# Spacing the last group's routing pieces and the final norm's steps between expert pairs

## The chip, the cores and the metric

The kernel runs on one core of one Trainium2 chip. Its time is the device time of one launch in microseconds (us), taken as the median of several runs. Engine names in the rows: PE is TensorE, DVE is VectorE, ACT is ScalarE, POOL is GpSimd, SP is SyncE; a small q behind a name is that engine's queue of DMA issues.

## The reference

One layer of a decoder trunk, in float32, for 1024 prompt tokens and 8 sample tokens of width 1024. The two groups share all weights.

```
n  = rmsnorm(x, g_mix) * (1 + sc1) + sh1            # adaLN
z  = n @ w_in                                        # conv branch, gMLP branch, two gates
x  = x + gt1 * ((sigmoid(g_a) * a + sigmoid(g_b) * b_br) @ w_out)
n2 = rmsnorm(x, g_ffn) * (1 + sc2) + sh2
q  = n2 @ w_q                                        # 8 heads, two half keys
s1, s2 -> top 16 of 128 each -> 256 sums -> top 16   # 128 experts per token
act = gelu(sum_d u_tab[eid] * n2)
x  = x + gt2 * sum_n (softmax gate * act)_n * v_tab[eid]_n
y  = rmsnorm(x, g_final)
```

The expensive part is the expert part. Every token reads 128 rows of `u_tab` and of `v_tab`, which lie side by side in memory as one row of 8 KB.

## The kernel before, in words

The tokens are cut into eight blocks of 128 (blocks 0 to 7) and one sample block of 8 (block 8). Three groups of blocks go through the dense front (norms, projections, convolution, gates, query, top 16): G1 is block 0, G2 is blocks 1 to 3, G3 (the last group) is blocks 4 to 8.

**Pairs.** The expert part is cut into pairs, counted by `at`. A pair is two gathers of 128 rows of 8 KB, 2 MB together. A block has 64 pairs (`PAIRS`), 32 for each half; the sample block has 4, ahead of block 7. That is 516 pairs: block 4 is pairs 256 to 319, block 5 is 320 to 383, block 6 is 384 to 447, the sample is 448 to 451, and block 7 is 452 to 515. For each pair:

- POOL issues two gathers into a slot (L1045, `fetch`). It first waits until PE has used the rows of the pair that had the slot before. Up to pair 255 there are three slots, from pair 256 (`WIDE_AT`) there are five.
- DVE multiplies each 128x1024 half by the token's vector and sums it (L1507, `dots`); ACT takes the gelu (L987); DVE makes the weights (L1524, `weigh`); PE multiplies the other half of the rows by them (L765, `value`), and so releases the slot.

**What stands between pairs.** Every engine's program is a fixed list in the order in which it is written. `beside_peer` (L370) writes it: `dots(at)`, `weigh(at)`, some steps of the fronts of G2 and G3 (over by pair 247), and then `extra(at)`. On DVE `extra` (L1608) issues three sorts of work:

- Routing pieces. `route` (L1432) turns the top-16 tables of one block into expert numbers and gates. It is a generator with ten pieces: piece 0 to piece 3 find the top 16 of 50 candidates for 8 heads; pieces 4 to 7 (the heavy ones) each have three instructions over 128x1600 elements (L1464, L1467, L1469), and piece 7 adds 16 small copies of `eid` (`to_quads`, L1429); piece 8 sums the softmax; piece 9 scales and makes 16 small copies of `gate`. Block 4 is routed in the front of G3. `routing_3` routes block 5, block 6, the sample (plus one piece, `to_slots`) and block 7, 41 pieces. They stand behind 10 consecutive pairs from pair 256, 10 from pair 320, and 21 from pair 384.
- `take_acc` takes the sum of a half out of PE's accumulator, two pairs behind its end.
- `early_norm` does the final norm of the blocks that are done: eight `x2` steps (L1552, the residual sum), mean squares, root, eight `y` steps (L1563). One step stands behind each pair from pair 452.

ACT does the exponential of each routing at pairs that the table `exps` names, and `square` and `root` of the norm at pairs counted from `last_block`. SP waits for the last routing (L476), then reads the eight 512 KB blocks of `x1_rows` and the sample's rows back, as `early_norm` needs them, and writes each `y` out once it is ready (L484).

Of the kernel before, what the change touches and what calls it, by code (L numbers as in the profile page):

```python
# [29 lines left out]
NB = NP // P  # L30
# [18 lines left out]
PAIRS = NSLOT * P // (2 * P)  # L49
# [2 lines left out]
NPAIRS = NB * PAIRS + SPAIRS  # L52
SAMPLE_AT = (NB - 1) * PAIRS
ROUTE_PIECES = 10
HEAVY = 3
END_B = 60
END_C = 4 * PAIRS - 8
# [38 lines left out]
def half_start(h):  # L96

    return HALF * h + (SPAIRS if h >= 2 * (NB - 1) else 0)
# [18 lines left out]
def build(nc, t):  # L117
# [3 lines left out]
    with ctx:  # L121
# [3 lines left out]
        def part(area, at, *shape):  # L125
            names = "abc"[:len(shape)]
            spec = "p (%s) -> p %s" % (" ".join(names), " ".join(names))
            return area[:, at:at + int(np.prod(shape))].rearrange(spec, **dict(zip(names, shape)))
# [112 lines left out]
        def width(b):  # L241
            return P if b < NB else NS


        def group(n, blocks, tg, xn, tables):
            g = Group()
            g.n, g.blocks, g.nb, g.tg, g.xn = n, blocks, len(blocks), tg, xn
            g.nt = sum(width(b) for b in blocks)
            g.ng = g.nt // tg
            g.nf = sum(b < NB for b in blocks)  # L250
            g.np = g.nf * P
            g.S = {k: S[f"{k}{1 if n < 3 else 2}"] for k in group_names}
            g.S |= {k: S[f"{k}{n}"] for k in ("x_in", "out_x1")}
            g.base = totals(G1) if n == 2 else {}

            g.order = list(range(g.nb)) if n < 3 else [0, 1, 2, 4, 3]
            g.cand = part(tables, 0, g.nb * H, NC)
            g.cid = part(tables, g.nb * H * NC, g.nb * H, NC)
            g.posf = part(mbuf, 3200, g.nb * H, TOP) if n < 3 else part(mbuf, 0, g.nb * H, TOP)
            g.crep = part(mbuf, 3200 + 512, H, NC) if n < 3 else part(mbuf, 1024, H, NC)  # L260
            g.eq = eq if n < 3 else part(mbuf, 2048, 2, TOP, NC)
            g.gt1 = (gt1_a, gt1_b, gt1_c)[n - 1]
            return g
# [3 lines left out]
        G3 = group(3, list(range(NB1, NBT)), 260, xn2, wring)  # L267
# [68 lines left out]
        def front_weights(g):  # L336

            for work, idle in ((4 * CC * g.ng, 5), (2 * CC * g.ng, 5), (4 * g.nb, 12), (2 * g.nb, 5),
                               (3 * KC * g.ng, 5), (2 * g.ng, 17), (3 * KC * g.ng, 7), (8 * g.nb, 3)):
                if work == 4 * CC * g.ng:  # L340
                    yield from norm_steps(g)
                    yield from [1] * 5
                yield from [HEAVY] * work
                yield from [1] * idle
            yield from norm_steps(g)
            yield from [1] * 5
            yield from [HEAVY] * (2 * g.nb)
            yield from [1] * 3
            yield from [HEAVY] * (NCH * (2 * g.ng + 1))
            yield from [1] * (2 * g.ng + 1) * 3  # L350
# [38 lines left out]
        def x1_again(b):  # L389
            return mbuf[:, b * D:(b + 1) * D] if b < NB1 else wring[:, (b - NB1) * D:(b - NB1 + 1) * D]  # L390
# [8 lines left out]
        def _(sp):  # L399
# [4 lines left out]
            def load(n):  # L404
                kind, src, col, _, _ = pieces[n]
                if user_ahead[n] is not None:
                    done, count = pieces[user_ahead[n]][3:]
                    sp.wait_ge(done, count)
                sp.dma_start(home(n), src[col]).then_inc(s_piece[slot_of[n]], 16)
# [78 lines left out]
        def _(pe):  # L488
# [292 lines left out]
            def begin(at):  # L781
                b, _, m = place(at)
                if b is None:
                    while made[0] < min(NS, max(3, 2 * m + 2)):
                        sample_x(made[0])
                        made[0] += 1
# [4 lines left out]
        def _(act_):  # L791
# [12 lines left out]
            def replicate(h, c):  # L804

                b, half = h // 2, h % 2
                j, q = 2 * half + c // NQ, c % NQ
                if c == 0:
                    g = G1 if b == 0 else G2 if b < NB1 else G3
                    act_.wait_ge(*g.to("n2_done", b - g.blocks[0] + 1))  # L810
                    if h >= 2:
                        act_.wait_ge(S["dots"], half_start(h - 2) + HALF)
                xn = xn1[:, b, :] if b < NB1 else xn2[:, b - NB1, :]
                made = ac(xr[QUAD * q:QUAD * (q + 1), j, :], xn[QUAD * j:QUAD * (j + 1), :], ACT.Copy)  # L814
                if c == 7:
                    made.then_inc(S["xr_ready"], 1)
# [172 lines left out]
            def square(n):  # L989

                b = finals[n]
                w = width(b)
                act_.wait_ge(S["x2_done"], n + 1)
                if n >= 2:
                    act_.wait_ge(S["fin_sq"], n - 1)
                ac(part(w2, 0, 2, D)[0:w, n % 2, :], x1_again(b)[0:w, :], ACT.Square, accum_out=stat[0:w, 0, n:n + 1]
                   ).then_inc(S["fin_sq"], 1)

            def root(turn, lo, hi):
                act_.wait_ge(S["fin_ms"], turn)  # L1000
                ac(stat[:, 1, lo:hi], stat[:, 0, lo:hi], ACT.Sqrt).then_inc(S["fin_root"], 1)

            exps = {PAIRS + ROUTE_PIECES * i + 6: G2 for i in range(2)}
            exps |= {at + 6: G3 for at in (4 * PAIRS, 5 * PAIRS, 6 * PAIRS, 6 * PAIRS + ROUTE_PIECES + 1)}
            copies = {half_start(h - 1) + 20 + c: (h, c) for h in range(2, 2 * NB) for c in range(8)}
            last_block = half_start(2 * (NB - 1))

            def extra(at):
                if at in exps:
                    next(exps[at].numerators)  # L1010
                if at in copies:
                    replicate(*copies[at])
                n = at - last_block - 4
                if 0 <= n < NB:
                    square(n)
                if n == NB + 1:
                    root(1, 0, NB)

            beside_peer(gelu, lambda at: None, {2: front(G2), 3: front(G3)}, extra)
            square(NB)  # L1020
            root(2, NB, NBT)
# [51 lines left out]
        def _(dve):  # L1073
# [457 lines left out]
            def take_acc(n):  # L1531

                dve.wait_ge(S["rows_used"], ends[n] + 1)
                for h in range(2):
                    part_ = slice(512 * h, 512 * (h + 1))
                    if n == 2 * (NB - 1):
                        out, acc, by = xn2[0:NS, 4, part_], ps[QUAD * h:QUAD * h + NS, 0, :], gts[:, part_]
                    else:
                        b, half = (n - (n > 2 * (NB - 1))) // 2, (n - (n > 2 * (NB - 1))) % 2
                        at = slice(2 * QUAD * half, 2 * QUAD * (half + 1))  # L1540
                        by_half = slice(2 * QUAD * h, 2 * QUAD * (h + 1))
                        out = (xn1[at, b, part_] if b < NB1 else xn2[at, b - NB1, part_])
                        acc, by = ps[by_half, half, :], gt2[by_half, part_]
                    last = v.tensor_tensor(out, acc, by, ALU.mult)
                last.then_inc(S["acc_read"], 1)
# [20 lines left out]
            def early_norm():  # L1566

                dve.wait_ge(S["x1_back"], 16 * NBT)
                dve.wait_ge(S["gfin_in"], 16)
                yield from gap(3)  # L1570
                dve.wait_ge(S["acc_read"], 2 * NB - 1)
                for n in range(NB):
                    x2(n)
                    yield
                yield
                mean_squares(1, 0, NB)
                yield from gap(2)
                dve.wait_ge(S["fin_root"], 1)
                rsqrt(0, NB)
                yield  # L1580
                for n in range(NB):
                    y(n)
                    yield
# [13 lines left out]
            def routing_2():  # L1597
                for i in (1, 2):
                    yield from route(G2, i)

            def routing_3():
                for i in range(1, 4):
                    yield from route(G3, i)
                yield from to_slots()
                yield from route(G3, 4)

            second, third, norms = routing_2(), routing_3(), early_norm()
            def extra(at):  # L1608
                if PAIRS <= at < PAIRS + 2 * ROUTE_PIECES:
                    next(second, None)  # L1610
                for b, count in ((4, ROUTE_PIECES), (5, ROUTE_PIECES), (6, 2 * ROUTE_PIECES + 1)):
                    if b * PAIRS <= at < b * PAIRS + count:
                        next(third, None)
                if at - 2 in ends:
                    take_acc(ends.index(at - 2))
                if at >= half_start(2 * (NB - 1)):
                    next(norms, None)

            dve.wait_ge(S["mask_made"], 1)
# [72 lines left out]
```

## Time and profile before

| | |
|---|---|
| median of 3 runs | 3551.34 us (3548.37 to 3553.54) |
| the profiled execution, its own time | 3556.78 us |
| its span | 3555.2 us |
| PE, DVE, ACT, POOL busy | 2051.7, 2448.6, 441.8, 1249.4 us |
| gathers (software queue) | 1082.20 MB of 1232.08 MB |
| share of the chain that ended last on DMA | 23% |

The execution has two regimes. Until about 2100 us the fronts of G2 and G3 run between the pairs, and no engine is full throughout. From there, in the last 17 of the 40 slices, only pairs, routing pieces and norm steps are left; DMA is full in most slices and below that in a few. A share over the whole span says little about the second regime, so it is read by stretches.

### The profile page before, as it was taken

How to read it: one execution, taken by the hardware profiler on the slowest of the kernel's cores; microseconds unless marked ns; L12 is line 12 of the kernel's file. 1: busy time of each engine (PE TensorE's matmuls, PEld its weight loads, DVE VectorE, ACT ScalarE, POOL GpSimd, SP SyncE). 2: the span in 40 equal slices, each digit the busy share in tenths (PEclk: the TensorE clock that was granted, in tenths of full speed). 3: DMA queues.
4: the chain of work that ended last, by engine and by line, in shares of the span. 5: the costliest groups of instructions: out<-in, count | busy, mean ns of one | idle time of the engine just before them, and what ended most of it. 6: DMA issues, size and time to landing. Idle time of an engine off the chain costs nothing. (4 is left out here: it accounts for less than half of the span.)

```text
span 3555.2 us, 28830 instructions
## 1 busy us (share of the span) xinstructions
PE 2051.7 (58%) x9548; PEld 995.9 (28%) x9548; DVE 2448.6 (69%) x6290; ACT 441.8 (12%) x1031; POOL 1249.4 (35%) x1046
## 2 busy tenths in 40 slices
PE   6873878986277777778688623333343333355333
PEld 4762444643144344455345300000000000000000
DVE  1447574479898796655768997766866697656665
ACT  1121101011111110110211011101010101011100
POOL 0001221222233433333434334544454444445343
PEclk9886988998588888899799855555555555555555
DMA  7734756798579999899999869999999998998998
GB/s 297 311 144 166 301 207 260 272 358 318 220 283 360 363 334 371 329 383 419 395 410 406 345 251 401 375 422 422 368 417 421 422 386 354 421 421 341 423 421 343
DMA packets 183925, 1232.08 MB, mean 347 GB/s; under 512 B 30512, under 2 KB 31152, under 8 KB 36320
## 3 DMA queue, kind: packets, MB, share of 16 engines
q0 software_dynamic: 148608, 1082.20, 75.9%
q1 hardware_dynamic: 35168, 148.05, 10.6%
q8 instruction: 75, 1.23, 0.1%
q14 instruction: 74, 0.61, 0.0%
HBM read 1221.14 MB, written 9.02 MB: 346 GB/s over the span
## 5 line engine op out<-in xcount | busy, mean ns | idle before, releaser
L1045 POOL DMA_INDIRECT big<-in_experts,eid x920 | 1112.0, 1209 | 2081.9 <-PE ps L765 1620.4
L1507 DVE SCALAR_TENSOR_TENSOR big<-big,xr 128x1024 f32<-128x1024 f32 x920 | 1113.6, 1225 | 525.3 <-DMA big<-in_experts,eid 520.2
L765 PE MATMUL ps<-big,wd 128*32 128x512 f32 x3680 | 726.2, 873 | 1089.8 <-DVE wd L1524 1085.2
L530 PE MATMUL ps<-big,wring 128*128 128x260 f32 (+2 forms) x2400 | 644.9, 423 | 81.5 <-issue 56.3
L530 PEld LDWEIGHTS ps<-big,wring 128*128 128x128 f32 x2400 | 447.6, 201 | 318.7 <-issue 166.1
L765 PEld LDWEIGHTS ps<-big,wd 128*32 128x32 f32 x3680 | 85.0, 127 | 1591.0 <-DVE wd L1524 1535.7
L987 ACT ACTIVATE gel<-act 128x2 f32<-128x2 f32 x516 | 105.7, 205 | 2569.9 <-DVE big L1507 2322.8
L1524 DVE TENSOR_SCALAR wd<-mask,gel,gate 128x32 f32<-128x32 f32 x1024 | 275.1, 363 | 152.3 <-ACT gel L987 141.5
L765 PE MATMUL ps<-w,wd 128*32 128x512 f32 x208 | 100.3, 1061 | 174.7 <-DVE wd L1524 170.8
L1205 DVE SCALAR_TENSOR_TENSOR arena<-arena,wdw 128x128 f32<-128x128 f32 (+2 forms) x360 | 182.9, 572 | 0.0
L682 PE MATMUL ps<-wring,mbuf 128*128 128x256 f32 (+1 forms) x528 | 128.6, 400 | 11.6 <-DMA wring<-in_w_out 6.3
L682 PEld LDWEIGHTS ps<-wring,mbuf 128*128 128x128 f32 (+1 forms) x528 | 96.0, 186 | 54.7 <-issue 28.8
L530 PE MATMUL ps<-arena,wring 128*128 128x260 f32 (+1 forms) x384 | 107.1, 422 | 0.0
L1045 POOL DMA_INDIRECT w<-in_experts,eid x52 | 57.2, 1100 | 130.3 <-PE ps L765 126.3
L765 PE MATMUL ps<-arena,wd 128*32 128x512 f32 x208 | 100.3, 1061 | 0.0
L1507 DVE SCALAR_TENSOR_TENSOR arena<-arena,xr 128x1024 f32<-128x1024 f32 x52 | 63.7, 1226 | 50.6 <-DMA arena<-in_experts,eid 50.6
L765 PEld LDWEIGHTS ps<-w,wd 128*32 128x32 f32 x208 | 10.2, 140 | 264.8 <-DVE wd L1524 259.2
L530 PEld LDWEIGHTS ps<-arena,wring 128*128 128x128 f32 x384 | 71.5, 190 | 37.9 <-issue 15.1
L1507 DVE SCALAR_TENSOR_TENSOR w<-w,xr 128x1024 f32<-128x1024 f32 x52 | 63.7, 1225 | 19.8 <-DMA w<-in_experts,eid 19.5
L1507 DVE DVE_READ_ACCUMULATOR big<-big,xr 128x1 f32 x920 | 76.8, 84 | 0.0
L1045 POOL DMA_INDIRECT arena<-in_experts,eid x52 | 68.6, 1319 | 15.9 <-issue 15.9
L814 ACT ACTIVATE xr<-arena 32x1024 f32<-32x1024 f32 x64 | 67.5, 1055 | 1.5
(219 smaller groups left out, 1881.0 us busy)
## 6 DMA issues: line engine op xcount, KB each, us to landing
wring<-in_w_in SPq DMA_DIRECT2D x40, 1024.0 KB
wring<-in_w_q SPq DMA_DIRECT2D x19, 1024.0 KB
big<-in_experts,eid POOLq DMA_INDIRECT x920
wring<-in_w_ada SPq DMA_DIRECT2D x12, 1024.0 KB
wring<-in_w_out SPq DMA_DIRECT2D x9, 1024.0 KB
big<-in_w_ada SPq DMA_DIRECT2D x6, 1024.0 KB, 6.9
xr<-in_w_ada SPq DMA_DIRECT2D x6, 1024.0 KB, 8.8
big<-in_w_in SPq DMA_DIRECT2D x4, 1024.0 KB, 14.7
```

Source lines behind the costliest of these rows:

```text
L530: mm = mmul(out, piece(n)[:, c, col:col + P], src[:, c, gi * tg:(gi + 1) * tg], start=(c == 0), stop=(c == k - 1))
L682: mm = mmul(ps[0:w, 2 + i % 6, 0:256], mT[:, c, cols(b)], piece(n + col)[:, c, :], start=(c == 0), stop=(c == KC - 1))
L765: mm = mmul(ps[QUAD * j:QUAD * (j + 1), half, :], wd[:, 2 * (at % 4) + jj, :], row(2 * slot + jj)[:, D + 512 * h:D + 512 * (h + 1)], start ...
L814: made = ac(xr[QUAD * q:QUAD * (q + 1), j, :], xn[QUAD * j:QUAD * (j + 1), :], ACT.Copy)
L987: ac(gel[:, c:c + 2], act[:, c:c + 2], ACT.Gelu).then_inc(S["gelu"], 1)
L1045: gp.indirect_dma_start(row(r), None, t["experts"], bass.IndirectOffsetOnAxis(ap=index, axis=0)).then_inc(s_row[r], 16)
L1205: ins = v.scalar_tensor_tensor(out=y, in0=aT[:, c, kk:kk + g.np], scalar=wdw[:, c, kk:kk + 1], in1=y, op0=ALU.mult, op1=ALU.add)
L1507: last = v.scalar_tensor_tensor(out=row(r)[:, 0:D], in0=row(r)[:, 0:D], scalar=1.0, in1=x, op0=ALU.mult, op1=ALU.mult, accum_out=act[:, c: ...
L1524: last = v.tensor_scalar(wd[:, c, :], mask[:], gel[:, c:c + 1], gate[:, b % 4, 2 * half + jj, m:m + 1], ALU.mult, ALU.mult)
```

## The change

The last group's 41 routing pieces no longer stand behind consecutive pairs in three bunches. One stands behind every fourth pair from pair 256 on (`ROUTE_STEP` = 4): block 5 at pairs 256 to 292, block 6 at 296 to 332, the sample at 336 to 372, `to_slots` at 376, block 7 at 380 to 416. The steps of the final norm stand behind every second pair from pair 452 (`NORM_STEP` = 2) instead of behind every pair, so the first `x2` is behind pair 458 instead of 455 and the last `y` behind 496 instead of 474. ACT's exponentials, squares and root move with them. No instruction is added or removed. From line 55 on, line numbers are two higher.

```diff
+ROUTE_STEP = 4
+NORM_STEP = 2
...
-            exps |= {at + 6: G3 for at in (4 * PAIRS, 5 * PAIRS, 6 * PAIRS, 6 * PAIRS + ROUTE_PIECES + 1)}
+            exps |= {4 * PAIRS + ROUTE_STEP * (at + 6): G3 for at in (0, 10, 20, 31)}
...
-                n = at - last_block - 4
-                if 0 <= n < NB:
-                    square(n)
-                if n == NB + 1:
+                n, rest = divmod(at - last_block - 1, NORM_STEP)
+                if rest == 0 and 3 <= n < NB + 3:
+                    square(n - 3)
+                if rest == 0 and n == NB + 4:
                     root(1, 0, NB)
...
-                for b, count in ((4, ROUTE_PIECES), (5, ROUTE_PIECES), (6, 2 * ROUTE_PIECES + 1)):
-                    if b * PAIRS <= at < b * PAIRS + count:
-                        next(third, None)
+                if at >= 4 * PAIRS and at % ROUTE_STEP == 0:
+                    next(third, None)
                 if at - 2 in ends:
                     take_acc(ends.index(at - 2))
-                if at >= half_start(2 * (NB - 1)):
+                if at >= half_start(2 * (NB - 1)) and (at - half_start(2 * (NB - 1))) % NORM_STEP == 0:
                     next(norms, None)
```

VectorE's list at two heavy routing pieces of block 5 before the change (`L1507 ... x2` and `L1524` are one pair; `mbuf`, `wring` and `eid_s` belong to the routing piece):

```order
L1464 TENSOR_TENSOR mbuf<-mbuf,iota 128x1600
L1467 TENSOR_TENSOR mbuf<-mbuf,wring 128x1600
L1469 TENSOR_REDUCE eid_s<-mbuf 128x32
L1507 SCALAR_TENSOR_TENSOR big,act<-big,xr 128x1024 x2
L1524 TENSOR_SCALAR wd<-mask,gel,gate 128x32 x2
L1464 TENSOR_TENSOR mbuf<-mbuf,iota 128x1600
```

The same two pieces on VectorE in the changed kernel:

```order
L1466 TENSOR_TENSOR mbuf<-mbuf,iota 128x1600
L1469 TENSOR_TENSOR mbuf<-mbuf,wring 128x1600
L1471 TENSOR_REDUCE eid_s<-mbuf 128x32
L1509 SCALAR_TENSOR_TENSOR big,act<-big,xr 128x1024 x2
L1526 TENSOR_SCALAR wd<-mask,gel,gate 128x32 x2
L1509 SCALAR_TENSOR_TENSOR big,act<-big,xr 128x1024 x2
L1526 TENSOR_SCALAR wd<-mask,gel,gate 128x32 x2
L1509 SCALAR_TENSOR_TENSOR big,act<-big,xr 128x1024 x2
L1526 TENSOR_SCALAR wd<-mask,gel,gate 128x32 x2
L1509 SCALAR_TENSOR_TENSOR big,act<-big,xr 128x1024 x2
L1526 TENSOR_SCALAR wd<-mask,gel,gate 128x32 x2
L1466 TENSOR_TENSOR mbuf<-mbuf,iota 128x1600
```

Between the two heavy pieces there was one pair and there are four now.

VectorE's list at the first steps of the final norm before the change, in block 7 (`L1552` is an `x2` step):

```order
L1552 TENSOR_TENSOR mbuf<-mbuf,xn 128x1024
L1507 SCALAR_TENSOR_TENSOR big,act<-big,xr 128x1024 x2
L1524 TENSOR_SCALAR wd<-mask,gel,gate 128x32 x2
L1552 TENSOR_TENSOR mbuf<-mbuf,xn 128x1024
L1507 SCALAR_TENSOR_TENSOR w,act<-w,xr 128x1024
```

The same steps on VectorE in the changed kernel:

```order
L1554 TENSOR_TENSOR mbuf<-mbuf,xn 128x1024
L1509 SCALAR_TENSOR_TENSOR big,act<-big,xr 128x1024 x2
L1526 TENSOR_SCALAR wd<-mask,gel,gate 128x32 x2
L1509 SCALAR_TENSOR_TENSOR big,act<-big,xr 128x1024 x2
L1526 TENSOR_SCALAR wd<-mask,gel,gate 128x32 x2
L1554 TENSOR_TENSOR mbuf<-mbuf,xn 128x1024
```

Two pairs stand between two steps instead of one, and the first step comes three pairs later.

## Rows read from the trace of the kernel before

**Rows 1.** The page: the span in 40 slices.

```profile
DMA  7734756798579999899999869999999998998998
GB/s 297 311 144 166 301 207 260 272 358 318 220 283 360 363 334 371 329 383 419 395 410 406 345 251 401 375 422 422 368 417 421 422 386 354 421 421 341 423 421 343
```

**Rows 2.** Stretches: length, PE, PEld, DVE, ACT, POOL busy, PEclk, DMA share, GB/s.

```profile
2285.00:2489.00 204.00, 79.31 (x328) 8.26 (x328) 124.70 (x248) 24.14 (x56) 96.61 (x82) 0.50 1.01 421
2164.70:2275.00 110.30, 38.32 (x160) 3.82 (x152) 92.77 (x233) 6.78 (x22) 49.59 (x39) 0.50 0.93 379
2496.90:2605.00 108.10, 38.36 (x160) 3.83 (x152) 92.16 (x232) 6.78 (x22) 48.81 (x39) 0.50 0.92 374
2827.20:2980.00 152.80, 50.17 (x212) 5.23 (x208) 141.36 (x365) 17.21 (x38) 67.21 (x51) 0.50 0.90 363
2980.00:3020.00 40.00, 12.83 (x56) 1.21 (x48) 18.93 (x37) 3.55 (x9) 15.68 (x14) 0.50 1.02 417
```

**Rows 3.** Stretches of block 5, L1507 alone, four records a pair: DVE busy, GB/s.

```profile
2496.90:2827.20 330.30, 156.69 (x256) 0.50 0.98 406
2497.00:2568.00 71.00, 24.01 (x40) 0.50 0.89 360
```

**Rows 4.** Timeline of one undisturbed pair: start, length, engine, instruction, [idle before, releaser].

```profile
3507.04 0.56 DVE L1524 TENSOR_SCALAR wd<-mask,gel,gate 128x32 f32<-128x32 f32 x2 [0.27 <-ACT gel L987]
3507.65 1.94 PE L765 MATMUL ps<-big,wd 128*32 128x512 f32 x8 [3.03 <-DVE wd L1524]
3508.01 1.23 DVE L1507 SCALAR_TENSOR_TENSOR big<-big,xr 128x1024 f32<-128x1024 f32 x1 [0.41 <-DMA big<-in_experts,eid]
...
3509.89 0.94 POOL L1045 DMA_INDIRECT big<-in_experts,eid  x1 [2.32 <-PE ps L765]
3510.50 1.23 DVE L1507 SCALAR_TENSOR_TENSOR big<-big,xr 128x1024 f32<-128x1024 f32 x1 [1.26 <-DMA big<-in_experts,eid]
...
3512.01 0.56 DVE L1524 TENSOR_SCALAR wd<-mask,gel,gate 128x32 f32<-128x32 f32 x2 [0.27 <-ACT gel L987]
```

**Rows 5.** Timeline of block 6's routing: a `take_acc`, heavy piece 5, the copies of piece 7.

```profile
2507.86 1.39 DVE L1544 TENSOR_TENSOR arena<-ps,gt 64x512 f32<-64x512 f32 x2
...
2531.87 1.82 DVE L1464 TENSOR_TENSOR mbuf<-mbuf,iota 128x1600 f32<-128x1600 f32 x1
...
2533.73 1.82 DVE L1467 TENSOR_TENSOR mbuf<-mbuf,wring 128x1600 f32<-128x1600 f32 x1
2534.26 2.11 POOL L1045 DMA_INDIRECT big<-in_experts,eid  x1 [5.28 <-PE ps L765]
2535.59 1.82 DVE L1469 TENSOR_REDUCE eid_s<-mbuf 128x32 f32<-128x1600 f32 x1
...
2554.71 3.05 DVE L1429 CAST eid<-eid_s 32x32 uint32<-32x32 f32 x16
```

**Rows 6.** Stretches of one pair each, L1507 alone: length, DVE busy, GB/s.

```profile
2528.81:2537.44 8.63, 2.38 (x4) 0.50 1.01 420
...
2546.07:2557.80 11.73, 2.38 (x5) 0.50 0.75 283
...
2561.42:2568.09 6.67, 2.38 (x5) 0.50 0.41 133
...
2571.16:2574.22 3.06, 2.37 (x4) 0.50 1.01 426
```

**Rows 7.** L1045, all gathers: from issue to landing.

```profile
DMA to landing us min/median/max: 7.5/19.2/24.0
```

**Rows 8.** Block 7: stretches with norm steps and without, all engines, GB/s last.

```profile
3230.00:3240.00 10.00, 5.34 (x32) 1.13 (x32) 9.18 (x19) 0.70 (x4) 6.28 (x5) 0.83 0.97 369
...
3290.00:3350.00 60.00, 20.42 (x88) 2.00 (x80) 40.34 (x70) 7.33 (x15) 21.23 (x21) 0.50 1.01 424
3350.00:3500.00 150.00, 58.05 (x240) 6.04 (x240) 91.99 (x182) 9.32 (x33) 69.51 (x61) 0.50 1.01 422
```

**Rows 9.** Timeline: the first `x2` step.

```profile
3236.16 1.22 DVE L1552 TENSOR_TENSOR mbuf<-mbuf,xn 128x1024 f32<-128x1024 f32 x1
```

## The prediction

> **What bounds the kernel now.** I read four views, in this order. First the span in slices [rows 1]: from slice 25 on (each slice is 88.9 us) DMA stands at 9 tenths and about 420 GB/s, with dips to 375, 368, 386 and 354; the 341 of slice 37 is the sample block, and the last slice holds the tail. So in this last part the gathers set the pace, and the question is what makes the dips. Second, one undisturbed pair on the timeline [rows 4]: the weights are made at 3507.04 and again at 3512.01, a period of 4.97 us, and both dot products sit behind a landing DMA (0.41 and 1.26 us of idle time). VectorE has room there. How much it has is seen where it does not wait for data: a pair without a piece then takes 3.06 us [rows 6]. The room is 4.97 - 3.06 = 1.91 us in each pair.
>
> Third, stretches around the three bunches [rows 2]. In quiet stretches DMA moves 421 GB/s. Around the bunches it moves 379, 374 and 363, and VectorE is busy 92.77 of 110.3, 92.16 of 108.1 and 141.36 of 152.8 us. Here VectorE is the bound: piece 5 in one pair makes it 8.63 us long, piece 7 11.73 us and piece 9 6.67 us [rows 6]. Less 3.06 that is 5.57, 8.67 and 3.61 us of piece, against 1.91 of room. Fourth, how VectorE's lateness reaches DMA. A slot is released by PE, PE waits for the weights, POOL waits for PE (2.32 us idle, then two issues) [rows 4]. A late dot product is a late gather five pairs on. But gathers wait in a queue: from issue to landing it takes 19.2 us in the median and 7.5 at the least [rows 7]. That is 11.7 us of reserve. Block 5 shows the reserve at work: its first ten pairs take 71.0 us instead of 49.7, so VectorE is 21.3 us late [rows 3], while DMA loses 12.1 us (below). 9.2 us were absorbed. I use 9.2, the smaller figure.
>
> **The change part by part.**
>
> *Routing pieces of blocks 5, 6, the sample and 7.* Nothing is added, so the gathers' bytes stay, and what can be won is the time in which DMA moved less than 421 GB/s [rows 2]:
> - bunch at pair 256: (421 - 379) / 421 x 110.3 = 11.0 us
> - bunch at pair 320: (421 - 374) / 421 x 108.1 = 12.1 us
> - double bunch at pair 384: (421 - 363) / 421 x 152.8 = 21.1 us, and 0.4 us for the 40 us behind it at 417
>
> The sum is 44.6 us. A second count agrees for the middle one: block 5's 64 pairs take 330.3 us [rows 3], and 64 x 4.97 = 318.1, a difference of 12.2.
>
> Do the spread pieces hide? A heavy piece makes VectorE late by 5.57 - 1.91 = 3.66 us; the next three pairs give back 3 x 1.91 = 5.73, so it is level again before the next piece. Piece 7 makes it late by 8.67 - 1.91 = 6.76; 1.03 is left three pairs on, and piece 8 is light. Piece 9 costs 3.61, gone after two pairs. `take_acc` (1.39 us [rows 5]) falls one pair behind a piece at pairs 289, 321, 353, 385 and 417; the worst is 321, behind heavy piece 6: 3.66 + 1.39 - 1.91 = 3.14. The peak is 6.76 us. Gathers are issued that much later at most, and the queue's reserve of 9.2 us covers it. Cost: nothing.
>
> POOL makes the margin smaller. Its issue at 2534.26 takes 2.11 us beside the two-input L1467 instead of the 0.94 of a quiet one [rows 4, 5], and it ends 0.82 us after L1467 does. One such stretch adds 1.17 us: 6.76 + 1.17 = 7.93, still under 9.2. The Trainium skill, "SBUF — State Buffer", section "SBUF: two separate sides", says that VectorE and GpSimd share a port pair by an exclusive lock, that a VectorE op with two SBUF inputs can take it for its whole length, and that GpSimd then cannot write descriptors and the DMA engines sit idle. The trace agrees as to the stretched issue; as to idle DMA it does not: in that very pair DMA moved 420 GB/s [rows 6].
>
> *ACT's exponentials.* Each stays six pieces behind the start of its routing, so VectorE meets it two pieces later, now eight pairs instead of two. No cost.
>
> *Reading x1 back.* SP waits for the last routing, which now ends behind pair 416 instead of 404. The norm needs the rows at pair 452, 36 x 4.97 = 179 us later. The bytes are the same and DMA is full at both places, so the price of these reads is unchanged and is not part of the 44.6.
>
> *Norm steps.* Eight `x2` steps of 1.22 us [rows 9] stood behind pairs 455 to 462, where VectorE is catching up after the sample. DMA moved 369 GB/s there from 3230 to 3240 us [rows 8]: (421 - 369) / 421 x 10 = 1.2 us at most could come back, and the first step starts only at 3236.16. Bounds: 0 and -1.2. I take -0.5. The eight `y` writes fall where DMA is full already (424 GB/s with them, 422 without [rows 8]); they cost their bytes and go on doing so until pair 496, with 19 pairs, 94 us, behind them. Nothing.
>
> **Sum.** 44.6 + 0.5 = 45.1 us. Against the profiled execution's own time: 3556.78 - 45.1 = 3511.7. That execution was 5.4 us above the median of 3551.34, so I forecast 3506.
>
> **Rivals.**
>
> 1. *POOL's lock shows.* If each heavy piece (four routings of four, 16) delayed a gather past the reserve by one stretched issue, 16 x 1.17 = 18.7 us would be left: 3525. For it: in the changed kernel heavy pieces stand beside issues all through 160 pairs. Against it: the 420 GB/s beside the first heavy pieces. This is what the skill's section named above would bring, if its idle DMA engines came about here.
>
> 2. *The reserve is gone (slower).* The 9.2 us may be a credit that only a full, undisturbed queue gives once per block, and that is empty when a piece comes every four pairs. Then each heavy piece costs its own peak less the reserve R. There are 13 heavy ones of 3.66 and 3 with copies of 6.76 (the sample has none). At R = 0 that is 13 x 3.66 + 3 x 6.76 = 67.9 us, against 44.6 won: 3551 + 23 = 3574. It decides from R below 1.4 us (13 x 2.26 + 3 x 5.36 = 45.5). For it: the delay of each heavy piece is real and comes 16 times instead of in three bunches. Against it: DMA has its 421 GB/s whenever VectorE is level, and it is level before each next piece, so the queue refills each time.
>
> 3. *The dips are not the pieces' doing.* If DMA slowed there for a reason of its own (the rows it reads, other traffic), moving the pieces brings nothing: 3551. For it: nothing but the fact that DMA is shared. Against it: VectorE's idle time vanishes in just these pairs, and DMA falls to 133 GB/s in a pair whose slots VectorE released late [rows 6].
>
> **How the numbers follow.** Forecast 84%, with its own range 3499 to 3514: the runs before spread by 5 us, the stretches' borders give 2 us either way, and exposed parts of the three pieces with copies could cost up to 5. Rival 1: 8%; rival 2: 4%; rival 3: 4%. The range for 8 in 10 is 3498 to 3518, which takes in rival 1 up to two thirds. A measurement can tell 0.2%, 7 us, from no change. Faster by more: forecast, rival 1 and a little of the rest, 0.93. Within it: 0.03. Slower: 0.04.
>
> **What would show it.** Right: the GB/s row reads about 420 in every slice from slice 26 to the end but the sample's and the last; VectorE's idle time before L1507 still ends with the DMA landing in the pairs without a piece; the sample's first pair starts about 44 us earlier; a heavy piece is followed by three pairs of which the first two are short. The x1 reads and y writes move but keep their lengths. Wrong: GB/s below 415 all through pairs 256 to 416 (rivals 1 and 2; with POOL issues of 2.1 us on the chain it is the first), or three dips left at the old pairs (rival 3). If the sample's dip (341 GB/s in its slice [rows 1]) gets deeper, part of the gain was lost again there, which I did not price.

## The result, and the profile after

| | before | changed |
|---|---|---|
| median | 3550.32 us (3548.37 to 3553.54, 4 runs) | 3517.44 us (3507.09 to 3523.17, 4 runs) |
| the profiled execution, its own time | 3556.78 us | 3523.17 us |
| its span | 3555.2 us | 3521.6 us |

The ratio is 0.9916, with a 95% interval of 0.9895 to 0.9937: 33 us faster, where 45 were forecast. The time lies 3.4 us above the forecast's own range (3499 to 3514) and just inside the one for 8 in 10 (3498 to 3518). One run of the kernel called lean below took 5273.89 us where its other three took 3512 to 3514; it is in no median and no ratio here. The span fell by 33.6 us. Where it went is read by the first dot products of four pairs: 256, 447 (the last of block 6), 453 (one behind the sample) and 515 (the last of all). The rows are VectorE's L1509 alone (L1507 before): stretch, length, VectorE busy, PEclk, DMA share, GB/s. First the kernel before:

```profile
2164.70:3173.90 1009.20, 466.78 (x764) 0.50 0.98 403
3173.90:3225.60 51.70, 14.67 (x24) 0.53 0.80 321
3225.60:3537.80 312.20, 152.37 (x248) 0.52 1.00 415
```

The changed kernel:

```profile
2167.20:3142.50 975.30, 467.30 (x764) 0.50 1.01 419
3142.50:3192.50 50.00, 14.69 (x25) 0.57 0.74 293
3192.50:3504.20 311.70, 152.40 (x248) 0.52 1.00 416
```

The 191 pairs from 256 to 447 gave 33.9 us, the sample's stretch 1.7 and block 7 0.5; pair 256 began 2.5 us later. 33.9 + 1.7 + 0.5 - 2.5 = 33.6. So the loss against the forecast lies in the 191 pairs, where it said 44.6.

Yet the signs I had named are mostly there. The page's slices of the changed kernel (DMA in tenths, then GB/s; each slice is 88.0 us):

```profile
DMA  7744756698669999899999977999999999998998
GB/s 298 303 158 155 298 208 259 265 353 316 244 259 356 384 309 369 333 370 419 416 403 407 381 291 320 421 422 421 419 421 422 421 415 402 419 404 347 422 423 342
```

Of the three dips of before [rows 1] two are gone; in place of the third, 354, slice 34 (2905 to 2993 us) still reads 402. The old bunches' stretches read 421, 419 and 406 against 379, 374 and 363 [rows 2], so by the forecast's own rule (421 - 406) / 421 x 153.1 = 5.5 us were still lost in the third. All engines, columns as in [rows 2]:

```profile
2167.30:2277.00 109.70, 42.10 (x176) 4.25 (x168) 80.31 (x201) 5.33 (x22) 50.44 (x43) 0.50 1.01 421
2489.90:2598.00 108.10, 42.33 (x176) 4.24 (x168) 83.45 (x194) 8.21 (x25) 49.90 (x44) 0.50 1.01 419
2812.90:2966.00 153.10, 59.20 (x248) 6.07 (x240) 122.00 (x273) 17.41 (x41) 70.36 (x60) 0.50 0.99 406
2409.40:2873.40 464.00, 177.95 (x740) 18.57 (x736) 346.20 (x808) 49.56 (x122) 217.55 (x184) 0.50 1.01 421
```

The last row holds the puzzle. It is pair 304 to pair 396: 92 pairs in 464.0 us, 5.04 us a pair. At the 4.97 of a full DMA [rows 4] they would take 457.4 (92 x 4.972). DMA's mean rate stood at its ceiling all the while, and the pairs still came 6.6 us late. Full by the mean is not full pace for the kernel.

Around a heavy piece the plan worked. The timeline of the changed kernel at pair 396 (start, length, engine, instruction, idle before and releaser):

```profile
2873.39 1.23 DVE L1509 SCALAR_TENSOR_TENSOR big<-big,xr 128x1024 f32<-128x1024 f32 x1 [0.42 <-DMA big<-in_experts,eid]
...
2875.88 1.23 DVE L1509 SCALAR_TENSOR_TENSOR big<-big,xr 128x1024 f32<-128x1024 f32 x1 [1.26 <-DMA big<-in_experts,eid]
...
2877.81 1.82 DVE L1466 TENSOR_TENSOR mbuf<-mbuf,iota 128x1600 f32<-128x1600 f32 x1
...
2879.66 1.82 DVE L1469 TENSOR_TENSOR mbuf<-mbuf,wring 128x1600 f32<-128x1600 f32 x1
2880.24 2.06 POOL L1047 DMA_INDIRECT big<-in_experts,eid  x1 [2.32 <-PE ps L767]
2881.52 1.82 DVE L1471 TENSOR_REDUCE eid_s<-mbuf 128x32 f32<-128x1600 f32 x1
2883.37 1.23 DVE L1509 SCALAR_TENSOR_TENSOR w<-w,xr 128x1024 f32<-128x1024 f32 x1
```

The pair with the piece takes 2883.37 - 2873.39 = 9.98 us, so VectorE is 9.98 - 4.97 = 5.0 us late, not the 3.66 I had. The 1.26 us wait for the second gather lies ahead of the piece and can't be used by it. The landed pairs that follow give the 5.0 back, and POOL's stretched issue (2.06 us) is there as expected. Hardly any of this reached the end, as the landings and the runs without the pieces show below.

### The profile page after: what moved, and what is told of

The parts are those of the page before. It is cut to its first block and busy times, and to the rows that moved or that the text cites. A ratio compares the mean times of both kernels' runs of the same rounds, so it can differ in the third digit from the quotient of the medians.

```text
span 3521.6 us, 28830 instructions
## 1 busy us (share of the span) xinstructions
PE 2047.3 (58%) x9548; PEld 993.7 (28%) x9548; DVE 2446.7 (69%) x6290; ACT 440.0 (12%) x1031; POOL 1230.9 (35%) x1046
## 5 line engine op out<-in xcount | busy, mean ns | idle before, releaser
L1047 POOL DMA_INDIRECT big<-in_experts,eid x920 | 1096.4, 1192 | 2071.1 <-PE ps L767 1613.0
L1509 DVE SCALAR_TENSOR_TENSOR big<-big,xr 128x1024 f32<-128x1024 f32 x920 | 1113.7, 1224 | 504.1 <-DMA big<-in_experts,eid 498.8
L684 PEld LDWEIGHTS ps<-wring,mbuf 128*128 128x128 f32 (+1 forms) x528 | 94.6, 184 | 51.7 <-issue 26.3
L1509 DVE SCALAR_TENSOR_TENSOR arena<-arena,xr 128x1024 f32<-128x1024 f32 x52 | 63.7, 1225 | 46.8 <-DMA arena<-in_experts,eid 46.6
L1509 DVE DVE_READ_ACCUMULATOR big<-big,xr 128x1 f32 x920 | 75.5, 82 | 0.0
L1509 DVE SCALAR_TENSOR_TENSOR w<-w,xr 128x1024 f32<-128x1024 f32 x52 | 63.6, 1223 | 14.4 <-DMA w<-in_experts,eid 14.1
## 6 DMA issues: line engine op xcount, KB each, us to landing
big<-in_experts,eid POOLq DMA_INDIRECT x920, 11.8
```

The costliest lines, as they stand in the source:

```text
L684: mm = mmul(ps[0:w, 2 + i % 6, 0:256], mT[:, c, cols(b)], piece(n + col)[:, c, :], start=(c == 0), stop=(c == KC - 1))
L1047: gp.indirect_dma_start(row(r), None, t["experts"], bass.IndirectOffsetOnAxis(ap=index, axis=0)).then_inc(s_row[r], 16)
L1509: last = v.scalar_tensor_tensor(out=row(r)[:, 0:D], in0=row(r)[:, 0:D], scalar=1.0, in1=x, op0=ALU.mult, op1=ALU.mult, accum_out=act[:, c: ...
```

## What the trace says of the single gathers

The rows above use DMA's mean over 16 engines. A gather's 128 rows are spread over all 16, and the dot product may start when the last engine has landed its share. So I counted, from the landing records of the trace, the time from the first to the last of the 16 landings of one gather near each of eight pairs (us; not a view of the profile):

```
pair            264  300  330  360  390  410  430  445
before          1.5  2.9  1.2  2.8  4.7  1.1  2.1  3.1
changed         2.1  4.9  6.0  7.9 10.9  9.0  7.3  8.2
```

Before, each bunch sets the spread back to 1 to 2 us: VectorE is late, gathers are issued late, the queues of all 16 engines run empty, and they start level again. In the changed kernel it grows until pair 400 or so. Near pair 390 (2858 us) the last engine lands 10.9 us after the first, but 8.3 us after the second-last: one engine lags, the other 15 do not. From there to pair 420 the spread falls to 7.3 us. The lagging engine does not catch up by itself in that stretch; the other 15 lose time there (the 406 and 402 GB/s above).

The last landing alone shows what sets the pace. In the changed kernel the last landings of consecutive gathers come 2.486 us apart (4.972 a pair), and they keep to that within 0.1 us over dozens of gathers. They fall behind it only in steps:

- 14 steps of 0.9 to 1.0 us (the first 0.7), 13 us together. All but the first come 1.5 to 2.3 us after an 8 KB refill of queue 14; between 2324 and 2839 us these are the refills at 2324, 2385, 2436, 2511, 2577, 2632, 2703, 2779 and 2839. The two others of that stretch, 2526 and 2645, leave the last landing as it is, and so do the 16 KB refills of queue 8, every 80 us.
- the `x1` reads between 2987 and 3025 us, 12.0 us together.
- three steps of 0.3 us at 2898, 2939 and 2962, while heavy pieces run and the spread is 9 to 11 us. no_heavy has none of them.

The last row of the stretches above is then no puzzle: seven such refills lie between pairs 304 and 396, 7 x 0.96 = 6.7 us, and 6.6 were missing.

The queues of the changed kernel in pairs 256 to 447 (queue, kind: packets, MB, share of 16 engines):

```profile
q0 software_dynamic: 55361, 403.14, 99.7%
q1 hardware_dynamic: 1312, 4.75, 1.2%
q8 instruction: 12, 0.20, 0.1%
q14 instruction: 19, 0.16, 0.0%
```

In the kernel before, the same 191 pairs saw less of the gathers pass:

```profile
q0 software_dynamic: 55108, 401.30, 96.6%
```

The difference is 1.84 MB or 4.4 us at 421 GB/s. I read it as the lead of the 15 engines over the one that lags: bytes moved ahead, which the kernel can't use.

This gave the theory that the later runs tested, named S in their expectations: the chain runs over the slowest engine. It pays the pairs' bytes, the `x1` reads, and about 1 us for each 8 KB refill of VectorE's instructions (the expectations say 1.0; the 0.94 used from here on was fitted on later runs, below). For the stretch from 256 to 447 of the changed kernel that is 191 x 4.972 (2.097 MB in 4.972 us is 421.8 GB/s) = 949.7, 4.75 MB at 421 = 11.3, and 1828 VectorE records / 128 = 14.3 refills x 0.94 = 13.4: together 974.4, against 975.3 measured. The rival, named R, was that VectorE's own lateness behind the spread pieces still cost what was missing.

## The experiments

All kernels are the changed kernel with an edit, except before_pad, which is the kernel before with one. "Stretch" is the time from pair 256's first dot product to pair 447's; the kernel before has 1009.2 us and the changed one 975.3. Medians are to be compared with the kernel before on the same chip: 3544.22 for the first four, 3543.99 for dve_pad to act_weights, 3545.71 for the last three.

**again.** The changed kernel once more, with no edit.

> The changed kernel once more, for its spread and a second trace. Two theories on the 11 us that were missing. Theory S (a lagging DMA engine): a gather is done when the slowest of 16 DMA engines has landed its rows; each 8 KB refill of VectorE's instructions (129 of its instructions, by 14 refills for some 1830) sets one engine back by 1.0 us, and without the bunches nothing lets it catch up. It expects the time from pair 256 to pair 447 at 975 us within 3 (191 x 4.97 + 11 for the x1 reads + 14 refills), and landings of one gather spread over 8 to 11 us near pair 390 as in the first trace. Theory R (the reserve runs out): VectorE is 5.0 and 8.1 us late behind heavy pieces, not 3.7 and 6.8, and holes in DMA of 7.5 us are the loss. It expects the same holes, wherever the engines stand. The time: 3507 to 3523 by both.

Measured: 3513.42 us (3506.73 to 3517.53, 6 runs), ratio 0.9911 (0.988 to 0.9942).

```profile
2160.90:3135.90 975.00, 467.05 (x764) 0.50 1.01 419
```

The stretch repeats to 0.3 us, and to 0.7 with route_only below; the two kernels with bunches, before and norm_only, differ by 1.9 us (1009.2 and 1007.3). Each kernel has one profile, so a difference of 1 us between stretches is near what can be told. What differs from run to run lies ahead of it: pair 256 began at 2160.9 here, at 2167.2 in the first profile.

**route_only.** The pieces spaced, the norm steps as before.

```diff
-NORM_STEP = 2
+NORM_STEP = 1
```

> Only the routing pieces are spaced, the norm steps stand behind every pair as before. Both theories: the routing has all of the gain and the norm nothing; within 2 us of the changed kernel in the stretch from pair 452 to the end, ratio to before 0.991 (0.989 to 0.993).

Measured: 3514.28 us (3510.16 to 3518.28, 7 runs), ratio 0.9916 (0.9891 to 0.994); stretch and block 7:

```profile
2157.10:3132.80 975.70, 467.06 (x764) 0.50 1.01 419
...
3179.60:3491.60 312.00, 152.34 (x248) 0.52 1.00 415
```

The whole gain is here.

**norm_only.** The norm steps spaced, the pieces in their bunches (ACT's exponentials too).

```diff
-            exps |= {4 * PAIRS + ROUTE_STEP * (at + 6): G3 for at in (0, 10, 20, 31)}
+            exps |= {at + 6: G3 for at in (4 * PAIRS, 5 * PAIRS, 6 * PAIRS, 6 * PAIRS + ROUTE_PIECES + 1)}
...
-                if at >= 4 * PAIRS and at % ROUTE_STEP == 0:
-                    next(third, None)
+                for b, count in ((4, ROUTE_PIECES), (5, ROUTE_PIECES), (6, 2 * ROUTE_PIECES + 1)):
+                    if b * PAIRS <= at < b * PAIRS + count:
+                        next(third, None)
```

> Only the norm steps are spaced, the routing pieces are bunched as before. Both theories: 0 to 1.3 us faster than before, ratio 1.000 (0.999 to 1.001). If it were slower by 3 us or more, the missing gain would lie in the norm.

Measured: 3546.22 us (3538.0 to 3551.56, 10 runs), ratio 1.0005 (0.9987 to 1.0023). Block 7 takes 312.2 us as before:

```profile
3207.10:3519.30 312.20, 152.50 (x249) 0.52 1.00 415
```

The norm steps are worth nothing that can be measured; I had taken 0.5 us. (Block 7 took 311.7 us in the changed kernel and 312.9 in again, so it repeats to 1.2.)

**no_heavy.** The three instructions over 128x1600 elements are left out of the last group's routings that `routing_3` does, 48 in all.

```diff
+                    if g.n < 3 or turn == 0:
+                        link(v.tensor_tensor(g.eq..., iota[:]..., ALU.is_equal))
+                        link(v.tensor_tensor(g.eq, g.eq, c_..., ALU.mult))
...
+                        link(v.tensor_reduce(eid_s[:, at]..., g.eq, AX.X, ALU.add))
```

> The changed kernel without the three large instructions of each heavy piece in the routing of blocks 5, 6, the sample and 7 (the expert numbers of block 4 are used again; the work left out is those 48 instructions). VectorE is then never more than about 3 us late. Theory S: the stretch from pair 256 to 447 stays at 972 to 976 us, as the refills stay (48 instructions of 1830 fewer), and the holes of single engines go without the pace getting faster; time within 3 us of the changed kernel. Theory R: the 7.5 us of holes come back, 967 us in the stretch and about 8 us less in time. The forecast as it was made: 964 us in the stretch.

Measured: 3511.48 us (3507.15 to 3525.85, 8 runs), ratio 0.9914 (0.989 to 0.9939).

```profile
2158.40:3132.40 974.00, 470.14 (x764) 0.50 1.01 421
```

Some 87 us of VectorE's heaviest work are gone (48 x 1.82), and the stretch is 1.0 to 1.7 us below those of again, changed and route_only. The heavy pieces of the changed kernel are all but hidden. The mean rate rose to 421: the time less the bytes at 421.8 GB/s was 7.4 us in the changed kernel and is 2.8 here (409.64 MB), so by my own rule 4.6 us should have come back. That rule falls here: the small holes of the mean fell to the 15 engines that were ahead, and the last one hardly lost by them. The spread is as large as with the pieces (11.9 us near pair 410).

**dve_pad.** Seven waits that are met long before, behind each pair from 256 on, on VectorE: instructions that do nothing but have to be fetched.

```diff
+                if at >= 4 * PAIRS:
+                    for _ in range(7):
+                        dve.wait_ge(S["consts"], 1)
```

> The changed kernel with seven more VectorE instructions behind each pair from 256 on, each a wait on a semaphore that was reached long before (about 0.02 us each, 0.15 us a pair against 1.9 us of room). They double the instructions of a pair. Theory S: 191 x 7 = 1337 instructions are 10.4 more refills at 1.0 us on the lagging DMA engine, so the stretch from pair 256 to 447 takes 985 us (983 to 987) in place of 975, and pairs 453 to 515 take 315 us in place of 312. Theory R: nothing, 975 and 312, since VectorE is late by 0.15 us more at most.

Measured: 3523.74 us (3516.24 to 3527.05, 5 runs), ratio 0.9942 (0.9923 to 0.9962). The stretch, block 7 and queue 14:

```profile
2154.70:3134.80 980.10, 466.39 (x765) 0.50 1.01 417
...
3186.50:3501.00 314.50, 152.46 (x248) 0.52 1.00 412
```

```profile
q14 instruction: 25, 0.20, 0.1%
```

The stretch missed both numbers: S had 983 to 987, R 975. In the trace the seven waits of a pair are about four records more (2550 against 1828, so 722 and not 1337). They brought 6 more refills, so one refill stands for about 120 to 128 of VectorE's records. Counted by records S gives 722 / 128 x 0.94 = 5.3 us more, and the stretch grew by 5.0 (0.9 us a refill); but this count was made after the run. Of the runs below, lean was forecast with it. Block 7 grew by 1.6 to 2.8 us with 2 more refills.

**act_pad.** The same seven waits on ScalarE.

```diff
+                if at >= 4 * PAIRS:
+                    for _ in range(7):
+                        act_.wait_ge(S["consts"], 1)
```

> The same seven waits behind each pair, on ScalarE, which is idle for 9 tenths. Theory S in its strict form, that each engine's instructions are refilled through a DMA engine of their own and the slowest sets the pace: ScalarE then has 12 to 13 refills against VectorE's 14, and the stretch stays at 975 (974 to 977). If both refills share one DMA engine: 985. If refills cost by their bytes spread over all 16 engines: 975.3 here and in the VectorE case too. Theory R: 975.

Measured: 3513.32 us (3506.99 to 3515.54, 4 runs), ratio 0.9913 (0.9888 to 0.9937).

```profile
2158.30:3133.30 975.00, 466.22 (x765) 0.50 1.01 419
```

```profile
q14 instruction: 25, 0.20, 0.1%
```

ScalarE has 974 records instead of 257 and queue 14 the same 25 refills, yet the stretch is unchanged. So it is not the refilled bytes as such. The landing records show where the difference lies. Eight of the 25 refills come every 120 to 143 us (2182, 2302, 2428, 2558, 2685, 2811, 2933, 3076), as 974 records at some 120 to 128 a refill would. None of the eight sets the last landing back: through the one at 2811 it keeps its place to 0.02 us, while VectorE's at 2830 sets it back by 0.94. ScalarE's refills do not fall on the engine that lands last. What they cost the engine that takes them the trace shows less clearly.

**split.** The three heavy instructions of a piece stand behind three pairs in a row, the copies of piece 7 behind the fourth, so VectorE is never more than one such instruction late.

```diff
+                    if g.n == 3 and turn:
+                        yield
                     link(v.tensor_tensor(g.eq, g.eq, c_.unsqueeze(2).broadcast_to([P, 2, TOP, NC]), ALU.mult))
...
-                if at >= 4 * PAIRS and at % ROUTE_STEP == 0:
+                if at >= 4 * PAIRS:
```

> The changed kernel with each heavy piece's three instructions behind three pairs in a row in place of one, and the 16 copies of the expert numbers behind the fourth. VectorE is never more than about 3 us late. Theory S: the stretch from 256 to 447 stays within 974 to 976. Theory R: 967 to 969.

Measured: 3512.08 us (3510.82 to 3512.52, 4 runs), ratio 0.991 (0.9889 to 0.9932).

```profile
2158.00:3132.90 974.90, 467.95 (x764) 0.50 1.01 420
```

R, which had 967 to 969, falls a second time: with the lateness cut into thirds, the stretch is the same.

**act_weights.** ScalarE makes the experts' weights in place of VectorE, in tiles counted by slot, so VectorE's list is shorter by the two scalings and two waits of each pair.

```diff
-                        last = v.tensor_scalar(wd[:, c, :], mask[:], gel[:, c:c + 1],
-                                               gate[:, b % 4, 2 * half + jj, m:m + 1], ALU.mult, ALU.mult)
...
+                for jj in range(2):
+                    last = ac(gg[:, c + jj:c + jj + 1], gel[:, c + jj:c + jj + 1], ACT.Copy,
+                              scale=gate[:, b % 4, 2 * half + jj, m:m + 1])
...
+                for jj in range(2):
+                    last = ac(wd[:, c + jj, :], mask[:], ACT.Copy, scale=gg[:, c + jj:c + jj + 1])
+                last.then_inc(S["weights"], 1)
```

> The changed kernel with the weights of a pair made by ScalarE (two products of gelu and gate, two of mask) in place of VectorE's two instructions, and with the tiles act, gel and wd counted by slot, which lets one wait of VectorE go. VectorE has 4 instructions a pair in place of 7. Theory S: in the stretch 256 to 447 VectorE needs 9.8 refills in place of 14.3 and ScalarE 10 to 12, so it takes 4 us less, 971 (969 to 972), and pairs 453 to 515 take 310.5 in place of 312. Theory R: the reserve lasts longer as VectorE has more room, 967 to 969. In the part before pair 256 VectorE gets 0.6 us a pair free, which no theory here prices.

Measured: 3491.89 us (3484.9 to 3494.48, 4 runs), ratio 0.9851 (0.9826 to 0.9875). VectorE has 1255 records in the stretch, three fewer a pair. The stretch and block 7:

```profile
2137.70:3108.50 970.80, 466.28 (x765) 0.51 1.01 420
...
3156.70:3472.30 315.60, 152.58 (x251) 0.51 0.99 410
```

The stretch hit its number (971). Block 7 did not: 315.6 where 310.5 were expected and the changed kernel has 311.7 (312.9 in again), which stays open. The larger gain is one I had not asked for: pair 256 begins at 2137.7, 17 to 30 us earlier than in the other kernels with spaced pieces. The fronts of G2 and G3 probably gain from VectorE's free time; no run tests that. A pair of this kernel on the timeline:

```profile
2407.45 0.20 ACT L1001 ACTIVATE gel<-act 128x2 f32<-128x2 f32 x1 [2.76 <-DVE big L1536]
2407.69 0.48 ACT L1009 ACTIVATE gg<-gel,gate 128x1 f32<-128x1 f32 x2
2408.20 0.53 ACT L1015 ACTIVATE wd<-mask,gg 128x32 f32<-128x32 f32 x2
...
2408.79 1.94 PE L771 MATMUL ps<-big,wd 128*32 128x512 f32 x8 [3.05 <-ACT wd L1015]
```

The weights are ready 1.3 us after the gelu starts, while VectorE needs 0.27 + 0.56 us behind it; in the stretch that delay does not show.

**before_pad.** The kernel before with the seven waits on VectorE: there the bunches reset the spread, so a refill could be free (S1 in the expectation) or be paid between the bunches (S2).

```diff
+                if at >= 4 * PAIRS:
+                    for _ in range(7):
+                        dve.wait_ge(S["consts"], 1)
```

> The kernel before (pieces in bunches) with the same seven waits of VectorE behind each pair from 256 on. Spaced, they cost 5.1 us in the stretch 256 to 447. Theory S1, that the lagging DMA engine catches up in each bunch: 0 to 1 us here, 1009 to 1010. Theory S2, that refills are plain work of that engine, hidden only where VectorE is late and the engine has nothing to do (about 300 of 1009 us): 0.7 x 5.1 = 3.6 us, 1012 to 1013.5.

Measured: 3551.44 us (3546.92 to 3559.12, 10 runs), ratio 1.0017 (1.0004 to 1.003).

```profile
2156.50:3170.20 1013.70, 466.78 (x764) 0.50 0.98 401
```

4.5 us more than before, 6.4 more than norm_only, which has the same bunches. S2 had 3.6 more, so this came out dearer, and S1 falls. The last landings fit a simple reason: outside the bunches and the reads they fall behind by 6.5 us in the kernel before and by 11.8 here. Behind a bunch the 16 engines are nearly level and another one lands last, so the first refills are hidden until VectorE's engine has overtaken it (before: no step at 2308, 0.36 us at 2398, 0.96 at 2488). Added refills come after that point and are paid in full.

**act_weights_2.** act_weights again, on another chip.

> The fastest version so far once more, for an interval: 3485 to 3495 us, ratio to before 0.985 (0.983 to 0.988); 970 to 972 us in the stretch 256 to 447, 315 to 316 in pairs 453 to 515.

Measured: 3494.14 us (3490.66 to 3498.34, 5 runs), ratio 0.9855 (0.9836 to 0.9875); stretch 970.7 us, block 7 315.9, pair 256 at 2140.7. Both the gain and the miss in block 7 repeat. This is the fastest version found, ahead of both kernels: 1.5% below before, 0.6% below the changed kernel's ratio.

**lean.** The tiles of `act`, `gelu` and weights counted by slot, so that VectorE needs one wait less per pair; nothing else moves.

```diff
-                c = 2 * (at % 4)
+                c = 2 * PLAN[at][0]
...
-                if at >= 4:
-                    dve.wait_ge(S["rows_used"], at - 3)
```

> The changed kernel with the tiles act, gel and wd counted by slot, so that VectorE's wait for the rows of three pairs before goes: one of its seven instructions a pair. Theory S: 191 instructions are 1.5 refills less, 973.5 us (973 to 974.3) in the stretch 256 to 447. Theory R: 975. If the waits were free because the engine takes them together with the next instruction: 975 as well, and VectorE's count stays at 1828.

Measured: 3512.51 us (3512.11 to 3513.83, 3 runs), ratio 0.991 (0.9882 to 0.9937); VectorE has 1637 records.

```profile
2158.90:3132.30 973.40, 466.81 (x764) 0.50 1.01 419
```

1.6 to 1.9 us less for 191 instructions less: small, at the edge of what can be told from one profile, and where it was expected (973.5).

The stretch of the kernels with spaced pieces against VectorE's records in it, and the account at 961.0 + 0.94 x records / 128:

| kernel | records | account | measured |
|---|---|---|---|
| act_weights | 1255 | 970.2 | 970.8 |
| lean | 1637 | 973.0 | 973.4 |
| no_heavy | 1764 | 974.0 | 974.0 |
| changed (again) | 1828 | 974.4 | 975.3 (975.0) |
| act_pad | 1828 | 974.4 | 975.0 |
| split | 1859 | 974.7 | 974.9 |
| dve_pad | 2550 | 979.7 | 980.1 |

961.0 is bytes alone (949.7 + 11.3); by the last landings the reads took 12.0. The 0.94 was fitted on lean and dve_pad, so these two rows do not test the slope; the other five lie 0.0 to 0.9 us above the account: (980.1 - 973.4) / (2550 - 1637) x 128. A line through these two meets zero instructions at 961.4, close to what the bytes need, though bytes had no part in the fit. The steps of about 1 us in the last landings can be counted as well: 9 in act_weights, 12 in lean, 14 in the changed kernel and 19 in dve_pad, where records / 128 gives 9.8, 12.8, 14.3 and 19.9.

## Why the prediction was off

**Right: what bounded it and the direction.** The dips were the bunches' doing, and they went with them. VectorE's lateness and POOL's stretched issues cost about 1 us together (rivals 1 and 2 do not hold), and rival 3 is refuted by route_only, where the gain came with the pieces alone. no_heavy and split bound what the spaced pieces still cost at 1 to 2 us in the stretch.

**Failed: "what can be won is the time in which DMA moved less than 421 GB/s".** This is the step of the 44.6 us; 33.9 came back in these 191 pairs. It reads a mean over 16 engines as if it were the rate of the kernel. One of them carries VectorE's refills and is set back 0.9 to 1.0 us by each. The last landings divide both stretches (us behind 2.486 a gather, net of a drift of some tenths):

| | before | changed |
|---|---|---|
| the three bunches | 11.3 + 10.4 + 18.8 = 40.5 | gone; 0.8 by heavy pieces |
| `x1` reads | 12.9 | 12.0 |
| refills, elsewhere | 6.5 | 12.8 |
| sum | 59.9 | 25.6 |

So two things were mis-sized. The bunches cost the last engine 40.5 us and not 44.6; I read the rest as idle time of the fast engines alone, while the slow one still worked. And 6.3 us of refills, which the bunches had hidden by setting all engines level, are paid once the bunches are gone. With the 0.8 of heavy pieces and 0.9 less for the reads, 10.3 of the missing 44.6 - 33.9 = 10.7 us are named. Why 8 KB set an engine back by 0.96 us was not found.

**Mis-sized with little effect.** The lateness behind a heavy piece is 5.0 us, not 3.66, since the wait for the second gather comes ahead of the piece; of it only the three steps of 0.3 us came through. The norm's 0.5 us did not show. The sample's stretch gave 1.7 us that I had not priced; it goes with a higher granted clock of TensorE there (below), and whether the change brought that is open.

**The sign that misled.** I had named "about 420 GB/s in every slice" as what shows the forecast right. It came true but for slices 33 and 34 (415 and 402) and slice 36 (404), in which the sample begins, and the forecast was off, because a rate of the mean can't tell 4.97 from 5.04 us a pair. Another sign could: the sample's first pair about 44 us earlier. Pair 447, the one before it, came 3173.9 - 3142.5 = 31.4 us earlier.

**Level of the run.** The forecast took 5.4 us off for the profiled run's place above its median. The profiled run of the changed kernel stood 5.7 above its own, so that term held, by luck: the one of norm_only stood 8.2 us below its median, that of route_only 3.7 below.

**Still open.** Why 8 KB cost an engine 0.96 us; which engine it is; which one takes ScalarE's refills, and at what price; why block 7 of act_weights is longer by 3 to 4 us; and what moves the start of pair 256.

## What to carry to other kernels

A stream over 16 DMA engines that must land whole goes at the pace of its slowest engine, so price a hole in it by what the slowest engine idles, by time per transfer and not by mean GB/s: look at the spread from the first to the last engine of one transfer before summing "lost bandwidth". A burst that stalls all engines also sets them level; whoever removes it pays the lag that it had hidden. Bursts that are spaced so that the engine is level again before the next one are nearly hidden if the queue holds several transfers, and the worth of each further refinement (a smaller piece, less work per piece) can be tested beforehand by leaving the work out. Once the stream is full, the number of instructions on an engine can matter though its busy time does not.

## What the runs showed of the hardware

- One DMA engine falls behind by 0.9 to 1.0 us with each 8 KB refill of VectorE's instructions, until it lands 10.9 us after the first (12.0 in dve_pad). 722 more instruction records cost 5 us of a stretch in which VectorE had time to spare (in the changed kernel it is busy 346.20 of the 464.0 us shown above). The same waits on ScalarE cost nothing, and its refills leave the last landing where it is.
- The length of the sample's stretch (pairs 447 to 453) goes with the granted clock of TensorE in it: 51.7 to 51.8 us at a mean of 0.53 (before, norm_only, before_pad, dve_pad), 48.2 to 50.0 at 0.57 (changed, again, lean, act_weights and its repeat) and 46.8 to 47.3 at 0.61 (route_only, no_heavy, act_pad, split). From route_only:

```profile
3132.80:3179.60 46.80, 14.68 (x24) 0.61 0.79 309
```

  All three kernels with bunches are at 0.53, but so is dve_pad, whose pieces are spaced; an effect of the spacing is neither shown nor excluded.
- With the same program up to there, pair 256 began anywhere between 2148.0 us (norm_only) and 2167.2 (changed). Most of the runs' spread lies there, and a difference of a few us between two medians says less than the stretch behind it, which repeats to 0.7 us with spaced pieces and to 1.9 with bunches.
